# Gate products of the latent and memory attention stages as three split products, with the weight halves made ahead; tanh moved behind the next exponentials in every attention stage

## What is computed

```python
for l in range(DEPTH):                                    # DEPTH = 2
    x = x + 0.5 * swiglu(rmsnorm(x, ffn1_norm[l]), w_ffn1_in[l], w_ffn1_out[l])
    u = rmsnorm(x, mix_norm[l])
    c_q, c_kv, k_r, hq, hf, hi, hgate, mq, gate_logits = split_sizes(u @ w_in[l], IN_SPLITS)
    y_mla = mla_branch(...) @ w_o_mla[l]                  # causal attention, 8 heads, from latents
    y_hg = hgrn2_branch(hq, hf, hi, hgate, lbs[l], hg_out_norm[l]) @ w_o_hg[l]
    y_mem = memory_branch(mq, rmsnorm(mem, mem_norm[l]), w_mem_kv[l]) @ w_o_mem[l]
    gates = jax.nn.sigmoid(gate_logits.reshape(B, S, N_BRANCH, D))
    merged = gates[:, :, 0] * y_mla + gates[:, :, 1] * y_hg + gates[:, :, 2] * y_mem
    x = x + merged @ w_out[l]
    x = x + 0.5 * swiglu(rmsnorm(x, ffn2_norm[l]), w_ffn2_in[l], w_ffn2_out[l])
```

## Time and profile before

| | us |
|---|---|
| median of 3 runs | 3035.98 (3032.4 to 3036.83) |
| the profiled execution | 3035.96 |
| its span | 3034.1 |
| TensorE busy | 2930.8 |
| VectorE busy | 1705.5 |
| ScalarE busy | 1183.8 |

### The profile page before, as it was taken

How to read it: one execution, slowest core, us unless ns; L and a number is a source line. 1 busy time by engine, 2 the same in 40 slices (tenths; PEclk the granted TensorE clock), 3 DMA queues, 4 the chain that set the end, 5 groups by cost and what they waited for, 6 DMA issues and landing times.

```text
span 3034.1 us, 49309 instructions
## 1 busy us (share of the span) xinstructions
PE 2930.8 (97%) x21248; PEld 2753.1 (91%) x21248; DVE 1705.5 (56%) x2866; ACT 1183.8 (39%) x1764; POOL 12.6 (0%) x20
## 2 busy tenths in 40 slices
PE   8998999999999899999999998999999999899998
PEld 8998788999999878899999996789989999678998
DVE  6667541566665743366666544446666653554665
ACT  5435421444444532244444323234454432332444
POOL 0000000000000000000000000000000000000000
PEclk9999999999999899999999998999999999999999
DMA  7543385555555243455564652445555465334553
GB/s 251 179 152 105 109 195 165 167 178 185 182 169 159 72 139 126 160 173 178 180 212 157 194 133 78 103 158 186 175 166 181 157 191 128 98 94 143 184 181 112
DMA packets 481272, 474.39 MB, mean 156 GB/s; under 512 B 47105, under 2 KB 464417, under 8 KB 480929
## 3 DMA queue, kind: packets, MB, share of 16 engines
q1 hardware_dynamic: 477472, 460.75, 48.6%
q0 software_dynamic: 3584, 10.49, 1.6%
HBM read 464.91 MB, written 6.29 MB: 155 GB/s over the span
## 4 chain that ended last, share of the span: by engine, by line
PE 90%; DVE 6%; ACT 3%; issue 1%; DMA 0%; DVEq 0%; SPq 0%; ACTq 0%
PE ps L825 32%; PE ps L924 31%; PE ps L945 16%; PE ps L978 4%; PE ps L1043 2%; DVE WL L1652 1%; PE ps L1018 1%; PE ps L868 1%; ACT WH L1337 1%; PE ps L872 1%; PE ps L876 1%; ACT REGION L1306 0%; PE ps L856 0%; DVE REGION L2018 0%; DVE TMP L2015 0%
## 5 line engine op out<-in xcount | busy, mean ns | idle before, releaser
L1652 DVE TENSOR_TENSOR WL<-RAW,WH 128x2048 fp32r<-128x2048 f32 (+1 forms) x342 | 762.4, 2234 | 447.7 <-ACT WH L1337 445.7
L1337 ACT ACTIVATE WH<-RAW 128x2048 fp32r<-128x2048 f32 (+1 forms) x342 | 631.5, 1857 | 148.7 <-DMA RAW<-in_w_in 54.6
L945 PE MATMUL ps<-HH,WH 128*128 128x256 f32 x1408 | 395.1, 281 | 2.3 <-DVE WL L1652 2.3
L945 PE MATMUL ps<-HH,WL 128*128 128x256 f32 x1408 | 395.5, 281 | 0.0
L945 PE MATMUL ps<-HL,WH 128*128 128x256 f32 x1408 | 394.7, 280 | 0.0
L924 PE MATMUL ps<-UH,WH 128*128 128x256 f32 x2688 | 378.5, 283 | 0.5 <-DVE WL L1652 0.5
L924 PE MATMUL ps<-UH,WL 128*128 128x256 f32 x2688 | 377.3, 283 | 0.0
L924 PE MATMUL ps<-UL,WH 128*128 128x256 f32 x2688 | 376.4, 282 | 0.0
L924 PEld LDWEIGHTS ps<-UH,WH 128*128 128x128 f32 x2688 | 346.2, 190 | 1.1 <-DVE WL L1652 0.7
L924 PEld LDWEIGHTS ps<-UL,WH 128*128 128x128 f32 x2688 | 346.7, 191 | 0.0
L924 PEld LDWEIGHTS ps<-UH,WL 128*128 128x128 f32 x2688 | 346.2, 190 | 0.0
(11 more groups left out here) (256 smaller groups left out, 3278.5 us busy)
## 6 DMA issues: line engine op xcount, KB each, us to landing
RAW<-in_w_ffn_in SPq DMA_DIRECT2D x88, 1024.0 KB, 5.1
RAW<-in_ffn_wi SPq DMA_DIRECT2D x88, 1024.0 KB, 5.1
RAW<-in_w_in SPq DMA_DIRECT2D x86, 1024.0 KB, 5.4
RAW<-in_w_ffn_out SPq DMA_DIRECT2D x32, 1024.0 KB, 5.1
RAW<-in_ffn_wo SPq DMA_DIRECT2D x32, 1024.0 KB, 5.2
RAW<-in_w_out SPq DMA_DIRECT2D x16, 1024.0 KB, 5.2
RAW<-in_w_ffn_out SPq DMA_DIRECT2D x16, 768.0 KB, 4.5
RAW<-in_ffn_wo SPq DMA_DIRECT2D x16, 768.0 KB, 4.4
```

The source lines that it names most:

```text
L945: last = nc.tensor.matmul(bank(n + side, 0, T), a[:, k, side * P:(side + 1) * P], b[:, k0 + k, :], start=k0 + k == 0 and a is wh and b is ...
L1337: nc.scalar.activation(split_ap(s, part_high(s)), raw_ap(s), ACT.Copy).then_inc(weights_high, 1)
L1652: v_.tensor_tensor(split_ap(s, part_low(s)), raw_ap(s), split_ap(s, part_high(s)).bitcast(FP), ALU.subtract)\
```

## The change

The gates of `mla` and `mem` become split products. TensorE waits for a slab's low half in place of its load. ScalarE and VectorE get `feed.to` calls: for slabs 0 and 1 of `mla` ahead of the stage (on VectorE in front of the merge of `hg.out`), for slabs 0 and 1 of `mem` among the copies of `mem.kv` (on VectorE behind the merge of `mla.out`), and for slabs 2 and 3 inside the stages, two slabs ahead of use. In every attention stage, those of the second stack too, the tanh of f[i] moves behind the exponentials of unit i+1.

```diff
+GATE_SPLIT = ("mla", "mem")
@@ the plan
-            pl.slab(f[m * ATTN[kind][0] // DK] + m % (DK // ATTN[kind][0]), places=places)
+            pl.slab(f[m * ATTN[kind][0] // DK] + m % (DK // ATTN[kind][0]), split=kind in GATE_SPLIT, places=places)
@@ TensorE, attention
-                            wait_weights(pe, sl)
-                            product(f[i + 1] + j, [(bank(f[i + 1] + j, 0, T),
-                                                    [(slot(sl, DK, 256)[:, k, m % 2 * P:(m % 2 + 1) * P], U[:, k, :]) for k in range(DK)])])
+                            cols = slice(m % 2 * P, (m % 2 + 1) * P)
+                            if kind in GATE_SPLIT:
+                                wait_split(pe, sl)
+                                terms = feature(parts(sl, DK, 256), UP, DK, cols)
+                            else:
+                                wait_weights(pe, sl)
+                                terms = [(slot(sl, DK, 256)[:, k, cols], U[:, k, :]) for k in range(DK)]
+                            product(f[i + 1] + j, [(bank(f[i + 1] + j, 0, T), terms)])
@@ ScalarE, attention
                     if i >= 1:
+                        for j in range(n_f):
+                            m = (i - 1) * n_f + j
+                            half_tanh(f[i - 1] + j, GATE[:, m, :], bank(f[i - 1] + j, 0, T))
+                    if i >= 1:
                         u = i - 1
...
-                    if i < units:
-                        for j in range(n_f):
-                            half_tanh(f[i] + j, GATE[:, i * n_f + j, :], bank(f[i] + j, 0, T))
+                    if kind in GATE_SPLIT and i < units and i % (2 // n_f) == 0:
+                        feed.to(slab_first[name] + min(3, i * n_f // 2 + 2))
@@ ScalarE, first stack
                 hg_gate(6, gate1 + 1)
+                feed.to(slab_first[L + "mla"] + 1)
                 attention(L + "mla", "mla", merged=L + "hg.out")
...
                         evict(n, MV[:, i % 2, c:c + 256], bank(n, 0, 256))
+                    if i in (3, 5):
+                        feed.to(slab_first[L + "mem"] + (i - 3) // 2)
@@ VectorE, attention
                     if i >= 1:
                         outputs(i - 1)
+                    if kind in GATE_SPLIT and i % (units // 4) == 0:
+                        feed.to(slab_first[name] + min(3, i * 4 // units + 2))
@@ VectorE, first stack
                 v_.tensor_tensor(MEM_SQ, MEM, MEM, ALU.mult).then_inc(squares_ready, 1)
+                feed.to(slab_first[L + "mla"] + 1)
                 merge(L + "hg.out", start=True)
...
                 merge(L + "mla.out")
+                feed.to(slab_first[L + "mem"] + 1)
                 attention(L + "mem", "mem", P ** -0.5)
```

## The result

| | before | after |
|---|---|---|
| median of 12 runs each, us | 3033.55 (3024.62 to 3037.28) | 3039.47 (3035.36 to 3044.24) |
| ratio, 95% interval | | 1.0024 [1.0015, 1.0032] |
| span of the profiled execution, us | 3034.1 | 3042.5 |

The change makes the kernel slower by 0.24%, which is 7.3 us, with an interval of 4.6 to 9.7. The predicted difference was +5.0 us, inside that interval; the predicted 3041.0 us lies 1.5 us over the measured median.

A forecast was written before the change was run, and what follows sets the result against it. TensorE, busy 97% of the span, was taken as the bound. Terms -9.1 (`mem`), +3.7 and +7.7 (`mla`), -1.7 and +4.4 (clock) sum to +5.0 on 3035.96, giving 3041.0 us; range 3031 to 3050.

The forecast's parts named there:

- The likeliest case: Whole kernel: the prediction's own sum, +5.0 us to 3041.0; chance 0.50 for 3037 to 3044.
- `mem`, both layers: Memory attention: shorter gate products with no new wait, -4.6 us each layer, -9.1 in all.
- entry wait, layers 0 and 1: Start of `mla`: TensorE's first scores wait 3.4 us for VectorE's first merge, held behind slab 1's subtraction.
- first transposes, each layer: `mla`, after the first gate product: TensorE waits 2.2 us for VectorE's scale_probs(0), late behind its eight merges.
- slab 3, layer 0, for o[2] and for t[3]: `mla`: slab 3's late load delays ScalarE's copy for o[2] by 3.7 us and VectorE's probabilities by 2.1.
- clock in `mla`, both layers: Falls of TensorE's clock at three long waits, 1.5 us each as the middle of 0 to 2.9: +4.4.
- the rival with 13.7 us: `mla`, layer 0: slab 3's load takes 13.7 us, ScalarE holds 4.4 us longer; total 3045 or 3048; chance 0.17.
- The price of a split product: Gate products of `mla` and `mem`: tanhs 2.88 us apart instead of 3.45, 0.57 less each, 18.2 in all.
- The rival by the clock: `mla`: TensorE at half rate from first wait to slab 3's last, +12.5 and +13.2, total 3050.9; chance 0.10.
- The -1.7: In front of `mem.kv`, layer 0: TensorE's 1.74 us wait vanishes because TensorE arrives nearly 8 us later.
- The tanh's worst case: Second stack, moved tanh: zero expected, at worst 0.4 us a unit, 13 us over 32 units.
- The last of the prediction's signs of being wrong: Second stack: the prediction is wrong if stages A, B or C move by more than 1 us.

The follow-up runs named there:

- e3: Changed kernel with VectorE's subtraction of slab 1 of `mla` moved behind the merge of `hg.out`; 3033.97 us, 0.9998 against before.
- e1: Kernel before with only the tanh moved behind the next exponentials in all attention stages, all gates full products; 3036.3 us, 1.0007 against before.
- e2: Changed kernel with split gates in `mem` alone, full products in `mla`; 3028.52 us, 0.9983 against before.
- e4: Changed kernel with `mla` slabs 1 to 3 split one slab ahead, not two, VectorE's subtraction between probabilities and output copy; 3027.64 us, 0.9982 against before.
- e6: Kernel before with GpSimd's eight writes of layer 0 spread: three beside `mla`, four in `mem`, one behind it; 3034.66 us, 0.9999 against before.
- e7: e4 with GpSimd's eight writes spread: three beside `mla`, the others released by products of `mem` and `mem.out`; 3019.39 us, 0.9945 against before.

## Why the prediction was right, and where it was not

**The forecast.** The likeliest case, +5.0 us, is what happened, and the stages it was made of gave +3.5 in the mean of three profiles. That the sum came out so near is in part luck: two of its terms missed by 6 us each, in opposite directions, and the +2.5 from elsewhere was in no term. It spoke of +0.2% as the border of what can be told, gave "same" 0.51 and "slower" 0.40; with 12 runs a side the loss of 0.24% turned out to be measurable. The terms, one by one:

| term | predicted | measured |
|---|---|---|
| `mem`, both layers | -9.1 | -9.2 |
| entry wait, layers 0 and 1 | 3.4 each | 3.09, 3.12 |
| first transposes, each layer | 2.2 | 0 |
| second transposes, each layer | 0.9 | 0.48 in layer 0, none in layer 1 |
| slab 3, layer 0, for o[2] and for t[3] | 3.7, 2.1 | 3.59, 1.82 |
| slab 3, layer 1 | 1.8 | 2.08 |
| all waits in `mla`, both layers | 20.6 | 14.2 |
| clock in `mla`, both layers | +4.4 | about +10.0 |
| `mem.kv`, layer 0 | -1.7 | -2.4 |
| tanh | 0 | 0 |

**What held.** The causes of the waits were right, engine by engine: the merge behind `take_low`, the copy for o[2] behind `feed_high`, VectorE late at slab 3. The load of slab 3 was put at 9.3 us from its neighbour and took 9.6, so the rival with 13.7 us did not come. The price of a split product was right too: tanhs in `mem` of after start 504.25 - 501.37 = 2.88 us apart, as in the earlier trace rows (others there stand 1.99 and 2.66 apart, since a tanh now also waits for the exponentials; the 4.6 us that the stage lost for 8 products are the surer reading).

```profile
501.37 0.38 ACT L1308 ACTIVATE REGION<-ps 128x256 f32<-128x256 f32 x1 [0.43 <-PE ps L826]
504.25 0.38 ACT L1308 ACTIVATE REGION<-ps 128x256 f32<-128x256 f32 x1 [2.50 <-PE ps L826]
```

**What was mis-sized.** The waits were put too long by 6.4 us in all, the clock too short by 5.6. One cause is behind most of both. After the entry wait the granted clock stood near the half level, in both layers:

```profile
396.40:400.20 3.80, 3.80 (x17) 3.44 (x17) 3.50 (x10) 0.44 (x3) 0.00 (x0) 0.55 0.39 136
...
404.00:415.00 11.00, 10.52 (x89) 9.73 (x87) 4.97 (x15) 1.75 (x6) 1.44 (x2) 1.00 0.92 208
...
417.00:427.20 10.20, 6.59 (x28) 5.83 (x29) 6.19 (x14) 4.58 (x17) 0.00 (x0) 0.51 0.89 195
1137.40:1144.00 6.60, 6.55 (x27) 6.22 (x28) 5.47 (x17) 2.95 (x6) 0.00 (x0) 0.50 0.24 85
```

While TensorE did its first scores and gate product at that rate, VectorE caught up, and the wait of 2.2 us before the first transposes turned into work at half speed. VectorE was also quicker than predicted: its eight merges in a row took 2.73 us, 0.34 each, where I had 0.45 each and 3.6 in all. The prediction said that a fall may pass inside the next wait. It did, the other way round: most of the wait passed inside the fall. `e3`, which has no entry wait and meets the first transposes at full clock, shows the wait of 1.96 us that was predicted as 2.2.

The clock's size follows from the budget. In layer 1 the waits of 5.2 us less the 4.6 saved leave +0.6, and the stage grew by 5.6, so 5.0 are the clock. The trace has 10.2 us at half level there, which is 5.1 us of lost work. In layer 0 it is 9.4 - (9.0 - 4.6) = 5.0, with 13.6 us at half level in the first profile, a part of them inside waits, and 10.2 in both repeats, where the stage is as long. I had taken 1.5 us at three places, the middle between no fall and the one of the earlier trace rows. Falls came in or behind every one of the waits of 3 us, in three profiles of three, and in layer 1 behind the wait of 2.08 too: four places at 2.5 us each. So the step that was mis-sized is the chance of a fall at each long wait, put at a half, and the number of such waits. The rival by the clock was nearer in mechanism than the chance of 0.10 that I gave it. The Trainium skill (TensorE: Matmul & The Clock Gate, "HAM oscillation") describes a kernel in which the matmuls behind every DMA wait, a longer wait than most of these, start at half rate. The trace agrees behind the waits of 3 us, but not behind that of 0.48, where the window from 404 on is at 1.00. The rival's size was off: its 25.7 us for `mla` stand against 15.0, since between the waits the clock was back at 1.00 (the window from 404 to 415).

**The -1.7.** Its direction was right, but it rested on a row that does not stay. Before waited there 1.74, 3.13 and 0 us in three profiles. The second:

```profile
453.23 2.04 PE L825 MATMUL ps<-REGION,RAW 128*128 128x256 f32 x4 [3.13 <-issue]
```

In e1 and e2, whose `mla` is before's, it was 0.99 and 3.32. That it vanishes when TensorE comes later held in all three profiles of after; that it grows when TensorE comes earlier is what e4 showed, with 5.04. The backlog did not end at about the same time as before, though, as the prediction has it: the load landed at 457.9 in after, 5.4 us later than in before, because the writes are released by the gate products of a stage that had got longer (the last was issued at 441.6, in before at 431.1). TensorE came 10 us later, so it found the load there all the same.

**The tanh's worst case** counts 32 units of the second stack. It has 48, 8 in each of A, B and C of both layers, so the bound should read 19 us; the measured term is nothing that shows.

**What was not foreseen.** The last of the prediction's signs of being wrong came: stretches that hold the stages of the second stack moved by more than 1 us (+4.1, -2.8, -1.6, +3.2), though the stages themselves did not. Nothing in the prediction let the clock change in stretches where TensorE's work stayed the same. It should at least have widened the range by the few us that this is worth in either direction.

## What to carry to other kernels

A helper's work that is made "ahead" has to be placed by what stands behind it on that helper's queue, not by how early its result is needed: one slab ahead with nothing urgent behind it was worth 13 us a layer-0 stage over two slabs ahead (64.3 against 77.7). When a stage gets shorter in front of a transfer that ends by its own backlog, move the transfer's competitors in the same change, or the gain is spent in waiting for it. And before a term is built on a single wait of a microsecond or two, profile the unchanged kernel a second time.

## What the runs showed of the hardware

- The granted clock falls with TensorE fully busy. At products of 32 matmuls with 30 or 24 columns it went to the half level for some us, with 80.00 of 80 us busy, in after at each of five, in the first profile of before at two of five. The neighbouring split products then ran at 0.21 us a matmul in place of 0.12.
- A spell at the half level outside a wait costs half its length: 3.4 us for 6.8 in `e3`, 5.0 for 10.2 in layer 1 of after.
- A wait of the same length need not bring a fall: 2.68 us in stage B of layer 0 did and 2.69 in layer 1 did not in before, while waits of 3.0 to 3.3 us at the entry of `mla` did each time, six times in the three profiles of after.
- The places of the falls between 1509 and 2257 us repeat in the changed kernel to 1 us over three profiles, 250 to 1000 us behind the last stage with split gates. Elsewhere its first profile differs (156 us at the half level in all, against 148 twice). In the kernel before, the first of three profiles differed. Runs of the kernel before, over 3024 to 3037 us, differ by more than the whole change, and most of that is the clock: among those beside the experiments, 3024.42 us has a granted clock of 0.983 and 3035.88 one of 0.979, which is 12 us of span.
- In and behind `mla`, a load of 1 MB took 4.7 to 5.6 us to land with no write of GpSimd's beside it, 5.6 to 6.2 with one of 640 KB (e6, e7), and up to 24.7 with several of them under way.
- Back to back, VectorE's eight merges of 128 x 256 took 2.73 us, 0.34 each, although one alone takes 0.42, as this row of before has it:

```profile
390.25 0.42 DVE L1753 SCALAR_TENSOR_TENSOR REGION<-REGION,ps 128x256 f32<-128x256 f32 x1 [1.30 <-PE ps L825]
```
